# Tile 3 and 4 gate products in smaller pieces, attention units and expert list 4 at other places in the run of experts

## The reference

```
proj = xn @ w_in                                   # q, k, v, gate (gu), value (gv) columns
attn = sliding-window attention with sinks         # units of four heads for tiles 2 to 4
sgu  = gelu(gu) * (w_spatial @ rms(gelu(gv)) + b)  # spatial gate
x    = x + concat(rms(attn), rms(sgu)) @ w_out
x    = x + memory_attention(rms(x))                # "cross"
q    = rms(x) @ w_peer_q                           # 8 heads, 2 halves of 128
s1,s2= top 16 of q_half @ sub_keys                 # a list: 16 experts of one head, per token
idx  = best 16 of the 256 pairs; gate = softmax
h    = u_tab[idx] . x ;  a = gelu(h) * gate
x    = x + sum_k a_k * v_tab[idx_k]
y    = rms(x)
```

## Time and profile before

| what | value |
|---|---|
| median of 3 runs | 1698.52 us |
| the profiled execution's own time | 1697.96 us |
| its span (first to last instruction) | 1696.2 us |
| PE, DVE, ACT, POOL busy | 77%, 69%, 48%, 39% |
| all DMA | 657.88 MB, 388 GB/s over the span |
| gathers and other POOL DMAs (queue 0) | 604.28 MB |

### The profile page before, as it was taken

How to read it: one execution, slowest core, us unless ns; L and a number is a source line. 1 busy time by engine, 2 the same in 40 slices (tenths; PEclk the granted TensorE clock), 3 DMA queues, 4 the chain that set the end, 5 groups by cost and what they waited for, 6 DMA issues and landing times.

```text
span 1696.2 us, 21662 instructions
## 1 busy us (share of the span) xinstructions
PE 1307.6 (77%) x7069; PEld 474.2 (28%) x7069; DVE 1165.1 (69%) x2798; ACT 806.8 (48%) x2337; POOL 656.4 (39%) x584
## 2 busy tenths in 40 slices
PE   9998987877888777678787776777677677766776
PEld 4454442333344222123232111212112111111110
DVE  2545749797667676777777677677666676777764
ACT  1424456774445454455555454445444445444443
POOL 0000234434534344444444444444444444444441
PEclk9999998989999788988988777877878877788865
DMA  9426799999999999999999999999999999999995
GB/s 359 165 100 251 274 388 420 414 374 421 420 421 421 417 394 414 422 405 412 421 420 421 421 421 421 421 422 420 421 421 422 421 406 421 422 421 420 421 418 220
DMA packets 97441, 657.88 MB, mean 388 GB/s; under 512 B 12512, under 2 KB 15584, under 8 KB 20768
## 3 DMA queue, kind: packets, MB, share of 16 engines
q0 software_dynamic: 83056, 604.28, 86.3%
q1 hardware_dynamic: 14272, 52.21, 8.0%
HBM read 653.24 MB, written 4.19 MB: 388 GB/s over the span
## 4 chain that ended last, share of the span: by engine, by line
DMA 44%; PE 25%; DVE 12%; ACT 11%; issue 7%; POOL 1%; ACTq 0%; DVEq 0%; POOLq 0%
DMA R<-in_peer_uv,R 42%; PE ps L2118 9%; PE ps L1624 5%; DVE R L1543 5%; PE ps L1878 3%; ACT L954 2%; ACT R L963 2%; ACT R L958 1%; PE ps L1595 1%; DVE R L1331 1%; ACT R L954 1%; DVE R L1332 1%; DVE R L1334 1%; ACT L862 1%; POOL R L684 1%
## 5 line engine op out<-in xcount | busy, mean ns | idle before, releaser
L2118 PE MATMUL ps<-R 64*64 64x512 f32 x4528 | 741.5, 736 | 355.8 <-ACT R L963 355.6
L684 POOL DMA_INDIRECT R<-in_peer_uv,R x566 | 643.6, 1137 | 830.7 <-PE ps L2118 754.1
L1543 DVE CUSTOM_DVE_ANT_0 R<-R 128x1024 f32<-128x1024 f32 x566 | 687.8, 1224 | 374.1 <-DMA R<-in_peer_uv,R 370.3
L954 ACT ACTIVATE R<-R 128x1 f32<-128x1 f32 x576 | 115.8, 201 | 602.0 <-DVE R L1543 600.7
L2118 PEld LDWEIGHTS ps<-R 64*64 64x64 f32 x4528 | 136.4, 151 | 710.2 <-ACT R L963 624.2
L963 ACT ACTIVATE R<-R 128x64 f32<-128x64 f32 x576 | 200.4, 348 | 54.9 <-ACT R L958 1.9
L1878 PE MATMUL ps<-A,R 128*128 128x256 f32 (+1 forms) x640 | 221.0, 470 | 0.7 <-ACT R L839 0.7
L958 ACT ACTIVATE R<-R 128x1 f32<-128x1 f32 x576 | 169.7, 295 | 20.9
L1878 PEld LDWEIGHTS ps<-A,R 128*128 128x128 f32 (+1 forms) x640 | 94.8, 198 | 256.1 <-issue 253.1
L1624 PE MATMUL ps<-A,R 128*128 128x512 f32 (+1 forms) x256 | 100.7, 545 | 0.4 <-ACT R L735 0.4
L1595 PE MATMUL ps<-R 128*128 128x256 f32 (+2 forms) x352 | 79.8, 382 | 0.0
(11 more groups left out here) (304 smaller groups left out, 947.5 us busy)
## 6 DMA issues: line engine op xcount, KB each, us to landing
R<-in_peer_uv,R POOLq DMA_INDIRECT x566, 15.6
A<-in_w_pq SPq DMA_DIRECT2D x8, 1024.0 KB, 9.8
A<-in_w_in SPq DMA_DIRECT2D x3, 2048.0 KB, 20.2
R<-in_w_out SPq DMA_DIRECT2D x4, 1024.0 KB, 9.0
x_res<-in_x_prompt SPq DMA_DIRECT2D x6, 512.0 KB, 8.6
R<-in_w_out_rows SPq DMA_DIRECT2D x1, 3072.0 KB, 9.9
R<-in_x_promptT SPq DMA_DIRECT2D x4, 512.0 KB, 7.3
R<-in_w_cq SPq DMA_DIRECT2D x2, 1024.0 KB, 10.7
```

Source lines behind the costliest of these rows:

```text
L684: pool.indirect_dma_start(slots[slot_of[g]], None, I["peer_uv"][:, :], bass.IndirectOffsetOnAxis(ap=idx[:, b % 4, k:k + 1], axis=0)).then_ ...
L954: act.activation(hgelu[:, b % 2, col], hdot[:, b % 2, col], ACT.Gelu).then_inc(gelu_ready, 1)
L1543: dve.tensor_tensor_reduce(u, u, xn(t), 1.0, 0.0, ALU.mult, ALU.add, hdot[:, b % 2, k:k + 1]).then_inc(u_used, 1)
L2118: ins = pe.matmul(bank(2 * (t % 2) + q)[rows], diag[tokens, g % DIAGS, :], v_rows[slot_of[g]][tokens, c * 512:(c + 1) * 512], start=first, ...
```

## The change

`UNIT_AT` goes from (24, 31, 38, 44, 51, 57) to (23, 32, 40, 45, 53, 58). `LATE[4]` goes from 8 to 5, so that every step of list 4 comes three experts sooner. The first entries of `PREP_AT`, `QUERY_AT`, `CROSS_AT`, `FFN_AT` go up by one. Tile 3's gate product is cut in 5 + 3 steps before experts 2 and 3 (was 8 before expert 2), tile 4's in 3 + 3 + 2 before experts 5, 6 and 7 (was 5 + 3 before 4 and 5); what follows them moves one or two experts later, and `half_T(4)` gets a PSUM bank of its own. Where a list's exponential and a unit's fall on the same expert, they are put side by side behind that expert's diagonal.

```diff
-        PREP_AT = {1: 1, 2: 122, 3: 200, 4: 210}
-        QUERY_AT = {1: 6, 2: 134, 3: 208, 4: 218}
-        CROSS_AT = {1: 9, 2: 138, 3: 222, 4: 244}
-        FFN_AT = {1: 28, 2: 158, 3: 268, 4: 16 * 23 + 2}
-        UNIT_AT = (24, 31, 38, 44, 51, 57)
+        PREP_AT = {1: 2, 2: 122, 3: 200, 4: 210}
+        QUERY_AT = {1: 7, 2: 134, 3: 208, 4: 218}
+        CROSS_AT = {1: 10, 2: 138, 3: 222, 4: 244}
+        FFN_AT = {1: 29, 2: 158, 3: 268, 4: 16 * 23 + 2}
+        UNIT_AT = (23, 32, 40, 45, 53, 58)
...
-        LATE = {2: 9, 4: 8, 12: 7}
+        LATE = {2: 9, 4: 5, 12: 7}
...
-            return 1 if t <= 2 else 5
+            return 1 if t <= 2 else 5 if t == 3 else 3
...
+            def exps_beside(g):
+
+                return any(g - at == 5 for at in UNIT_AT)
...
-                        if step == 21:
+                        if step == 21 and not exps_beside(g):
                             gates(n, n % 4)
...
-                    if g == 2:
+                    if g == 3:
                         gates_out(3)
-                    if g == 6:
+                    if g == 7:
                         gates_out(4)
-                    if g == 8:
+                    if g == 10:
+                        qkT_evac(3)
                         half_norm(3)
                         half_norm(4)
-                    if g == 9:
-                        qkT_evac(3)
...
                     for t, r, u, at in units():
+                        for n, step in query_steps(g):
+                            if step == 21 and g - at == 5:
+                                gates(n, n % 4)
                         unit(t, r, u, g - at)
...
-                elif g == 3:
+                elif g == 4:
                     gated(3)
-                elif g == 7:
+                elif g == 9:
                     gated(4)
-                elif g == 9:
+                elif g == 11:
                     half_rows(3)
                     half_rows(4)
-                elif g == 12:
+                elif g == 13:
                     half_take(3)
-                elif g == 13:
+                elif g == 14:
                     half_take(4)
...
-                if t > 1:
+                if t in (2, 3):
                     pe.wait_ge(h_T, t - 1)
...
-                    project(3, 2)
-                elif g == 4:
+                    project(3, 2, 0, 5)
+                elif g == 3:
+                    project(3, 2, 5, KD)
+                elif g == 5:
                     pe.wait_ge(sgu_out, 4)
-                    project(4, 2, 0, 5)
-                elif g == 5:
-                    project(4, 2, 5, KD)
+                    project(4, 2, 0, 3)
                 elif g == 6:
+                    project(4, 2, 3, 6)
+                elif g == 7:
+                    project(4, 2, 6, KD)
+                elif g == 8:
                     pe.wait_ge(pq_so, 2)
                     gating(4, bank(5))
-                elif g == 8:
+                elif g == 10:
                     pe.wait_ge(p_T, 3)
                     pe.wait_ge(sgu_out, TILES)
                     heads_T(3)
-                elif g == 10:
+                elif g == 11:
                     pe.wait_ge(qkT_out, 8)
                     heads_T(4)
-                elif g == 11:
+                elif g == 12:
                     pe.wait_ge(qkT_out, 10)
                     half_T(3)
                 elif g == 13:
                     half_T(4)
                 elif g == 14:
-                    pe.wait_ge(h_T, 4)
+                    pe.wait_ge(h_T, 3)
```

## The result

| | before | after |
|---|---|---|
| median of 4 runs | 1698.24 us (1696.72 to 1699.43) | 1711.68 us (1710.04 to 1714.12) |
| ratio, 95% interval | | 1.008 (1.0064 to 1.0096) |
| span of the profiled execution | 1696.2 us | 1711.0 us |
| PE, DVE, ACT, POOL busy | 77%, 69%, 48%, 39% | 77%, 68%, 47%, 38% |
| table loads on ACT | 140 | 136 |

The change is 0.8% slower, some 13.4 us, where I forecast 2.5 us faster with a range up to 1701. No engine has more instructions to do (PE 7069 in both). The first view is again the windows; the rows stand for the stretches of the earlier trace rows except 224 to 232 us, and for two more.

A forecast was written before the change was run, and what follows sets the result against it. Gathers on the DMA engines were taken to bound three quarters of the run. List 4's -2.5 us plus 0 for the start gave 1695.5 against the profiled 1697.96, or 1696.0 against the median 1698.52; range 1692.0 to 1701.0.

The forecast's parts named there:

- List 4: Hole at 360 to 368 us: earlier index wins 3.7 us, 1.2 us given back; sum -2.5 us, between -3.7 and 0.
- list 4's two `top_keys` fit: DVE, 330 to 348 us: it idles 6.1 us, so both `top_keys`, five instructions of about 0.34 us each, fit there.
- The give-back: After list 4's gain: 0.7 us lost before expert 74's gather, 0.5 us for expert 67's behind ACT's long block; 1.2 us.
- 4 us or more: Sign of being right: PE stands still some 4 us or more before expert 64, until L1325 ends near 377.
- The other shifts by one: Such as slot 7's first use behind tile 1's memory attention: cost nothing, at most 2.5 us each if gather cover is gone.
- The start: Before about 240 us: early holes won equal losses around 235; 0 us, between -2.4 and +4.
- (a): PE at expert 9: heads 2 and 6 issued four us later, landing at 226; stall 1.6 us, bounds 0 and 6.5.
- (b): ACT at expert 10 copies tile 3's heads before the two `half_norm`s: PE idles 3.1 us where it idled 2.6.
- The early pieces: Gate products cut finer free slots sooner, feeding the hole at 212 to 216 us: up to 1.8 us won.
- Table loads: ACT behind experts 45 and 58: 4 fewer loads at 1.28 us, 5.1 us less on ACT, adding nothing to the sum.
- keeps diagonals 60 to 63 from being late: What the ACT saving from fewer table loads does; the -2.5 us assumes it, and it adds nothing itself.
- the start turns into a stall: Rival, 0.18: heads 2 and 6 land 13.6 us after issue, PE stands 6.5 us; +3.5, or 1702.0 if list 4 wins nothing.

The follow-up runs named there:

- the first pair: Only units 0 and 1 moved, `UNIT_AT` (24, 31) to (23, 32), on the kernel before: ratio 1.0054 (1.0034 to 1.0074).
- the six: All six `UNIT_AT` entries at their new places, exponentials side by side, on the kernel before: 1.0032, also with `FFN_AT[1]` at 29.
- experiment 4: `UNIT_AT` moved on the kernel before: units 0 and 1 1.0054, 2 and 3 1.0030, 4 and 5 0.9987, all with `FFN_AT[1]` at 29 1.0032.
- the last pair: Only units 4 and 5 moved, `UNIT_AT` (51, 57) to (53, 58), on the kernel before: ratio 0.9987 (0.9974 to 1.0000).

## Why the prediction was wrong

**List 4 (forecast -2.5 us, measured +0.18%, 3 us slower).** The mechanism that was to be removed was read rightly: POOL's wait for the index went, and the hole at 360 with it. The step that failed is "list 4's two `top_keys` fit" into DVE's 6.1 idle us from 330 to 348. I summed idle time over a window, while DVE works in order: in the change both stand ahead of unit 1's `attn_take` (expert 53), with the list alone the first one does (expert 52), and PE waits for it: 5.44 us for 1.81. The earlier trace rows made me follow exactly this coupling for tile 3 and not for tile 2, two units before. The give-back was there too: in the kernel after, tile 3's `attn_take` starts at 392.00, right behind `best_pairs`, and PE's 4.50 us are the "4 us or more" that I gave as a sign. The index came at 359.9 with the list alone (355.5 forecast): I had left expert 57's product at 351.69, though `best_pairs` now stands ahead of it, and it started at 356.25. The give-back of 1.2 us had two terms, and both were too small in the kernel after: the 0.7 us behind unit 5's transposes became the hole at 392 to 400, (1.01 - 0.57) x 8 = 3.5 us, and the 0.5 us for expert 67's gather became POOL's 6.91 us, with a share of 0.66 from 380 to 384, 1.4 us.

**The units' new places (forecast 0, measured +0.32%, 5.4 us slower).** This is the largest miss. The sum has no term for them, except for unit 5's transposes in the list's give-back; the step that failed is "The other shifts by one [...] I cost at nothing: DMA stays at 1.01 over them, with several gathers in flight". With the units alone the share is 0.38 and 0.40 from 364 to 372 us and 0.06 from 392 to 396, and the bound of 2.5 us for each shift didn't hold either: the first pair, two shifts by one, costs 0.54%, 9.2 us, by itself. What the six cost beyond their gaps stays open (experiment 4). PE's in-order queue holds every expert behind the transposes; a wait there delays slots and so gathers eight experts later, and the next wait can come of it. The step asked what each move costs alone and not what its distance to its partners becomes.

**The start (forecast 0, between -2.4 and +4; measured +0.23%, 4 us slower).** The bounds held, if only just, the middle didn't. (a) PE's stall for the weights: 2.53 us after, 3.38 alone, for 1.6 taken. The later of the two loads took 8.6 us after and 9.5 alone, for the 8.2 that I took (217.8 to 226). SP issued them 1.3 us sooner than forecast in the kernel after, and PE got there 1.4 us sooner (223.07 for 224.5). The Trainium skill's "DMA: Bandwidth & Descriptors", section "Issuing engines are not separate DMA queues", says that loads and gathers interleave on the same engines. By that rule fewer gathers in flight mean a faster landing, and the traces agree as far as they go: 8.4 us in the median with the start alone, 7.6 after, for 11.4 in the one trace of before that has the figure. The DMA share during the landing was hardly lower, though (0.96 alone, 0.98 before). (b) PE idle behind ACT: 3.56 us for 3.1 forecast; that term was right. What I missed is that (a) and (b) stand in one row, weights, heads, norms, `half_T`, and each lateness is passed on whole: expert 18's gather went out at 243.47, 5.4 us later, where 2.1 was forecast. The early pieces gave what was hoped (212 to 216 at 0.90), but from 180 to 300 us together the kernel after loses 13.3 us for 10.5, which is less than two traces can differ by.

**Table loads (forecast 4 fewer, worth 0).** Right: 140 to 136. At 1.28 us each they would be 5.1 us. The price was too low: for the block behind expert 58 I took 6.3 us and left out its third load, back to Gelu. It took 7.67 us (368.48 to 376.15), and PE waits 3.32 us behind it (L936) before unit 4's transposes. So "keeps diagonals 60 to 63 from being late" failed. How much the exponentials side by side hold up ACT was not tried by itself.

**The sum and the rivals.** 3.9 + 3.1 + 5.4 = 12.4 us of 13.4. The rival "the start turns into a stall" had the right side, at 1702.0, and late gathers around 235 us, but not its condition: the weights landed within 10 us, and PE stood 2.53 us and not 6.5. It too took the other parts as 0. Of the three signs given as "wrong" one came true: a new hole of over 2 us between 370 and 400.

## What to carry to other kernels

Idle time in a window can be used only by work that stands at that place in the engine's own order; before an operation is moved, list every wait that its new place comes ahead of, on its engine and on the partner that waits for that. Where several engines run fixed tables side by side, what counts is the distance between partners (here `attn_take` and the transposes behind it) and who stands between them, so move a pair and not one of it, and try the parts apart: of the start, list 4 three experts sooner and the three pairs only the last pair was faster by itself, and its interval reaches 1.0000. A wait is worth removing only to the point where the next one takes over. Here list 4 one, two and three experts sooner gave ratios of 0.9996, 1.0012 and 1.0018, and with the last pair moved, one and two gave 0.9979 and 0.9976.

## What was not expected of the hardware

The clock makes PE's waits dearer than they read. Timeline of PE in the units alone, an expert's product and a unit's values:
```profile
369.71 1.98 PE L2125 MATMUL ps<-R 64*64 64x512 f32 x8 [1.46 <-ACT R L963]
...
377.51 3.67 PE L2094 MATMUL ps<-R 128*128 128x64 f32 x16
```
Here, at a granted clock of 0.50 to 0.59, the product takes 1.98 us and the sixteen matmuls of the values 3.67 us; at 1.00 (2.4 GHz) they take 1.09 and 1.89 us. The low level stood for over 12 us behind a gap of 3 us in which PE waited, though PE had work in all of the last eight. The kernel before has it too, 0.50 from 376 to 380 behind its wait of 4.93 us, but is back at 1.00 from 384 on. In the trace of the last pair the clock is 0.50 from 364 to 368 us and 1.00 from 372 on. I had costed PE's waits at their own length.
